# Moving three quarters of the second layer's routing beside the next block, with a ring of two weight strips in place of three

## The chip, the cores and the metric

The kernel runs on one core of one Trainium2 chip. The metric is device time in microseconds (us) of one execution; the median of three timed runs before the change is 1821.57 us (1821.03 to 1824.02).

## The reference

A two-layer decoder trunk on 256 tokens of width 1024, all in float32. Layer 0 mixes tokens with RWKV-7 and mLSTM heads; layer 1 with causal forgetting attention of 16 heads. Each layer is followed by PEER, an expert retrieval. For a block of 128 tokens it computes:

```
q  = (xb @ w_q)                      # 8 heads, two halves of 128
s1 = q half 1 . sub_k1 ; s2 = q half 2 . sub_k2    # 128 scores each
v1,i1 = top16(s1); v2,i2 = top16(s2)
sc,ci = top16(all 256 sums v1+v2)    # 16 experts a head, 128 a token
gate  = softmax(sc)
act   = gelu(xb . u_tab[expert])
out   = sum(gate * act * v_tab[expert])
```

The tables hold 16384 experts; a row of u and the same row of v stand side by side in memory, 2 x 1024 floats. Each of the 128 tokens of a block needs 128 such rows.

## The kernel before, in words

Five instruction streams run beside each other, ordered by semaphores, each written out in the order in which its engine works.

**Expert rows.** There are four expert passes, n = 0 to 3 (layer 0 blocks 0 and 1, layer 1 blocks 0 and 1), of 128 slots each. For each slot POOL issues one indirect DMA (L542) that brings one (u, v) row for each of the 128 tokens: 128 partitions x 8 KB, 1 MB, into a ring of 11 slots. DVE multiplies the u half with the tokens and sums (`Stream.dot`, L1700); ACT makes gelu, weight and a diagonal matrix of it (`Weights.pair`, L1201 to L1214); PE multiplies the diagonal matrix with the v half and adds into PSUM (`Experts.row`, L893), and by that frees the ring slot, for which POOL waits before it issues the row 11 further on. Each engine takes slots in pairs, by calls `ex.pairs(n)` that are strewn through the other work. PE runs one pair behind the count of ACT and DVE.

**Which pass runs beside what.** While layer 1's block b is mixed (`mixer1(b, ex)`, `mixer1_tail(b, ex)`), the pass n = 1 + b is streamed, that is the experts of the block before. The third, n = 3, runs alone at the end. In `mixer1` there is one pair for each of the 16 weight strips of q, k, v and the output gate, two pairs by the normalization of q and k ("rms"), and two for each of the eight attention steps. The tail has four pairs by the output projection, three at the layer norm, one at the first query strips, and three for each of four routing groups (`tail_pairs`); what is left of the 64 pairs goes in `finish()`.

**Routing.** `route(l, b, groups, between)` on DVE picks the experts. A group is two heads: top-16 of four score rows, 256 sums, top-16 again, indices by one-hot products, then `experts_chosen`, for which POOL's gather waits head by head. `between` is called at eight hooks of a group. ACT's counterpart is `gates` (an Exp for each group, after `gate_shifted`). Scores of all 16 half-heads of layer 1 go into `sc[:, 0]`, where they are read by `route`.

**Weights.** SP brings matrices as strips of 256 columns, 1 MB each, into the buffers of `wring`, WRING = 3 of them, used in turn. Strip i is loaded when the PSUM bank that was the last reader of strip i - WRING has been filled (L430). In layer 1 two strips fill one bank (`feature_strips`, `token_strips`): strip, pair, strip, bank filled, pair. So a bank's filling lets two loads go at once. In layer 0 most strips fill a bank of their own. `mixer0` begins the output projection with the mLSTM half of the rows of WRING strips before the RWKV half ("mixed") is ready; the transposes of the RWKV part stand before the last of them.

Of the kernel before, what the change touches and what calls it, by code (L numbers as in the profile page):

```python
# [58 lines left out]
PAIRS = tuple((2 * g, 2 * g + 2) for g in range(GROUPS))  # L59
FIRST_GROUPS = ((0, 1), (1, 2)) + PAIRS[1:]  # L60
# [17 lines left out]
def tail_pairs(g, hook):  # L78

    return int(hook in (0, 2, 5))  # L80
# [49 lines left out]
WRING = 3  # L130
# [68 lines left out]
def build(nc, T, out):  # L199
    ROWS, NROWS = parameter_rows()  # L200
    ctx = ExitStack()
    with ctx:
# [87 lines left out]
        ARENA = 36352  # L290
# [74 lines left out]
        keyT = cut(22528, 2048).rearrange("p (i n) -> p i n", i=16)  # L365
        qT = cut(24576, 4096).rearrange("p (i n) -> p i n", i=16)
        sc = cut(28672, 4096).rearrange("p (b i n) -> p b i n", b=NB, i=16)
        cand = cut(32768, 512).rearrange("p (h n) -> p h n", h=2)
        scr = cut(33280, 512)
        onehot = cut(33792, 512).rearrange("p (h k j) -> p h k j", h=2, k=TOPK)  # L370
        v16 = cut(34304, 64).rearrange("p (i k) -> p i k", i=4)
        i16f = cut(34368, 64).rearrange("p (h two k) -> p h two k", h=2, two=2)
        csc = cut(34432, 32).rearrange("p (h k) -> p h k", h=2)
        hilo = cut(34464, 64).rearrange("p (w h k) -> p w h k", w=2, h=2)
        e12 = cut(34528, 64).rearrange("p (w h k) -> p w h k", w=2, h=2)
        eidf = cut(34592, 32)
        gate = cut(34624, NB * SLOTS).rearrange("p (b s) -> p b s", b=NB)
        hid = cut(34880, NB * SLOTS).rearrange("p (b s) -> p b s", b=NB)
        ga = cut(35136, NB * SLOTS).rearrange("p (b s) -> p b s", b=NB)
        gsum = cut(35392, 2 * EH)  # L380
        uints = cut(35408, 416).bitcast(U32)
# [4 lines left out]
        diag = [cut(35840 + j * P, P) if j < 4 else early[:, (j - 4) * P:(j - 3) * P] for j in range(DIAGS)]  # L386
        qT1 = cut(24576, 2048).rearrange("p (i n) -> p i n", i=16)
# [3 lines left out]
        ogs = cut(24576, D)  # L391
        qc = cut(25600, 1024).rearrange("p (t n) -> p t n", t=8)
        kc = cut(26624, 2048).rearrange("p (t n) -> p t n", t=8)
        fv = cut(30720, 2048).rearrange("p (b n) -> p b n", b=NB)
        SQ = cut(28672, 2048).rearrange("p (t n) -> p t n", t=16)
        lg = cut(28672, 2 * 512).rearrange("p (j q n) -> p j q n", j=2, q=2)
        probT = cut(29696, 2 * 512).rearrange("p (j q s n) -> p j q s n", j=2, q=2, s=2)
        oT = cut(32768, D).rearrange("p (t n) -> p t n", t=KT)
# [153 lines left out]
        def _(pe):  # L552
# [25 lines left out]
            def mixer0():  # L578
# [192 lines left out]
                w = next_strip(pe)  # L771
                done(project_out(claim(pe, "mix_out", WRING), w, range(0, KT), True, True), "mix_out")
# [195 lines left out]
            def mixer1_tail(b, ex):  # L968
# [16 lines left out]
                for g in range(GROUPS + 1):  # L985

                    def between(j):
                        for i in (range(0, 2), range(2, 4))[j]:
                            ex.pairs(tail_pairs(g - 1, i) if g else QUERY_PAIRS * (i == 0))

                    if g < GROUPS:
                        k = EH + 1 + 4 * b + g
                        feature_strips("peer_q", k, b, between)
                        pe.wait_ge(S("peer_q_taken"), k + 1)
                        ps = claim(pe, "peer_s", k).rearrange("p (q n) -> p q n", q=4)
                        done(score_keys(ps, 0, range(4 * g, 4 * g + 4), lambda j: qT1[:, j, :]), "peer_s")
                        first_hook = 4
                    else:
                        first_hook = 0
                    if g:  # L1000
                        for i in range(first_hook, 8):
                            ex.pairs(tail_pairs(g - 1, i))
# [18 lines left out]
        def _(act):  # L1021
# [205 lines left out]
            def gates(n, groups, meanwhile):  # L1227

                for g, (h0, h1) in enumerate(groups):
                    for i in range(6):  # L1230
                        meanwhile(g, i)
                    gates_begun[0] += 1
                    act.wait_ge(S("gate_shifted"), gates_begun[0])
                    x = gate[:, n % NB, TOPK * h0:TOPK * h1]
                    af(x, x, ACT.Exp).then_inc(S("gate_exp"), 1)
                    for i in range(6, 8):
                        meanwhile(g, i)

            def mixer1(b, ex):
                tok = slice(b * P, (b + 1) * P)  # L1240
                wide = lambda ps: ps.rearrange("p (t n) -> p t n", n=P)
                take_x(4 + 4 * b, b)
                taken(af(fz, full(act, "fox_f", b)[:, 0:P], ACT.Identity, bias=small[:, 2:3], scale=1.0), "fox_f")
                ex.pairs(EARLY_PAIRS)
                for i in range(4):
                    ex.pairs(strip_pairs(2 * i))
# [9 lines left out]
                    ex.pairs(strip_pairs(2 * i + 1))  # L1256
                for i in range(2):
                    ex.pairs(strip_pairs(8 + 2 * i))
                    taken(copy(fv[:, b, i * 512:(i + 1) * 512], full(act, "fox_v", 2 * b + i)), "fox_v")
                    ex.pairs(strip_pairs(9 + 2 * i))  # L1260
                for i in range(12, 15):
                    ex.pairs(strip_pairs(i))
                for i in range(2):
                    taken(af(ogs[:, i * 512:(i + 1) * 512], full(act, "fox_og", 2 * b + i), ACT.Sigmoid), "fox_og")
                ex.pairs(strip_pairs(15))
# [25 lines left out]
            def mixer1_tail(b, ex):  # L1291
# [12 lines left out]
                def take_scores(g):  # L1304
                    ps = full(act, "peer_s", EH + 1 + 4 * b + g).rearrange("p (q n) -> p q n", q=4)
                    taken(copy(sc[:, 0, 4 * g:4 * g + 4, :], ps), "peer_s")

                def meanwhile(g, i):
                    ex.pairs(tail_pairs(g, i))
                    if g + 1 < GROUPS and i == 1:  # L1310
                        take_queries(g + 1)
                    if g + 1 < GROUPS and i == 3:
                        take_scores(g + 1)
# [4 lines left out]
                gates(2 + b, PAIRS, meanwhile)  # L1318
# [15 lines left out]
            ln_root(6)  # L1334
            ex.finish()
# [4 lines left out]
        def _(dve):  # L1340
# [277 lines left out]
            y_scratch = cut(25088, 1024)  # L1618
# [25 lines left out]
            def route(l, b, groups, between):  # L1644
# [10 lines left out]
                for g, (h0, h1) in enumerate(groups):  # L1655
# [6 lines left out]
                    top16(sc[:, 0 if l else b, js, :], scratch[:, 0:2 * nh, :], v16[:, 0:2 * nh, :], i16[:, 0:2 * nh, :], 2 * nh,  # L1662
# [83 lines left out]
            def mixer1(b, ex):  # L1746

                for i in range(2):
                    ex.pairs(strip_pairs(i))
                dve.wait_ge(S("fox_f_taken"), b + 1)  # L1750
                stt(fl, fz, -1.0, fz, ALU.mult, ALU.max).then_inc(S("f_abs"), 1)
                for i in range(2, 16):
                    ex.pairs(strip_pairs(i))
# [34 lines left out]
            def mixer1_tail(b, ex):  # L1788
# [10 lines left out]
                route(1, b, PAIRS, lambda g, i: ex.pairs(tail_pairs(g, i)))  # L1799
# [24 lines left out]
            layer_norm(6)  # L1824
            ex.finish()
# [50 lines left out]
```

## Time and profile before

| what | us |
|---|---|
| median of the timed runs | 1821.57 |
| the profiled execution | 1815.61 |
| its span, first to last instruction | 1813.6 |
| PE busy | 1551.5 |
| DVE busy | 1063.3 |
| ACT busy | 606.0 |
| POOL busy | 576.3 |

The page gives 40 slices of 45.3 us with the bytes moved in each. Expert rows are moved from about 325 us to about 1790 us. Layer 1's block 0 is mixed from about 680 us and its tail routes until about 1060 us; block 1 follows from about 1085 us to about 1465 us; the last pass takes the rest. SP's waits appear as SPq; a gather's issue has POOL's name.

### The profile page before, as it was taken

How to read it: one execution, taken by the hardware profiler on the slowest of the kernel's cores; microseconds unless marked ns; L12 is line 12 of the kernel's file. 1: busy time of each engine (PE TensorE's matmuls, PEld its weight loads, DVE VectorE, ACT ScalarE, POOL GpSimd, SP SyncE). 2: the span in 40 equal slices, each digit the busy share in tenths (PEclk: the TensorE clock that was granted, in tenths of full speed). 3: DMA queues.
4: the chain of work that ended last, by engine and by line, in shares of the span. 5: the costliest groups of instructions: out<-in, count | busy, mean ns of one | idle time of the engine just before them, and what ended most of it. 6: DMA issues, size and time to landing. Idle time of an engine off the chain costs nothing.

```text
span 1813.6 us, 18606 instructions
## 1 busy us (share of the span) xinstructions
PE 1551.5 (86%) x6020; PEld 927.1 (51%) x6020; DVE 1063.3 (59%) x2499; ACT 606.0 (33%) x1760; POOL 576.3 (32%) x561
## 2 busy tenths in 40 slices
PE   8999988998777778997899789998999787777775
PEld 7779877664222225753457436654557433222222
DVE  1683544577888865335557984325557985444444
ACT  1434311333333333236532332246632332222222
POOL 2000000344444442333332352234542354333330
PEclk9999859999999999999999999999999899999999
DMA  6222003999999999999999989999999899999996
GB/s 245 94 93 70 1 24 126 380 413 420 419 420 419 420 420 420 419 420 420 419 418 418 407 345 419 419 419 420 419 419 419 347 357 420 420 420 420 419 421 269
DMA packets 92063, 638.32 MB, mean 352 GB/s; under 512 B 11072, under 2 KB 13120, under 8 KB 15424
## 3 DMA queue, kind: packets, MB, share of 16 engines
q0 software_dynamic: 73728, 536.90, 71.9%
q1 hardware_dynamic: 18240, 100.24, 14.1%
q8 instruction: 49, 0.80, 0.2%
q14 instruction: 46, 0.38, 0.1%
HBM read 636.05 MB, written 1.05 MB: 351 GB/s over the span
## 4 chain that ended last, share of the span: by engine, by line
PE 45%; DMA 32%; DVE 15%; ACT 6%; issue 2%; POOL 0%; ACTq 0%; SPq 0%; DVEq 0%; POOLq 0%
DMA arena<-l_peer_uv,arena 31%; PE psum L893 19%; PE psum L575 12%; DVE arena L1700 6%; PE psum L874 4%; DMA wring<-l_w_in 2%; PE psum L752 1%; PE psum L797 1%; PE psum L668 1%; DVE arena L1639 1%; DVE arena L1630 1%; PE psum L658 1%; DVE arena L1631 1%; PE psum L667 1%; DVE arena L1635 1%
## 5 line engine op out<-in xcount | busy, mean ns | idle before, releaser
L542 POOL DMA_INDIRECT arena<-l_peer_uv,arena x512 | 563.1, 1100 | 1124.8 <-PE psum L893 870.2
L1700 DVE CUSTOM_DVE_ANT_0 arena<-arena,xres 128x1024 f32<-128x1024 f32 x512 | 617.8, 1222 | 454.8 <-DMA arena<-l_peer_uv,arena 452.3
L893 PE MATMUL psum<-arena,early 128*128 128x512 f32 x1024 | 487.9, 622 | 115.5 <-ACT early L1214 112.9
L893 PE MATMUL psum<-arena 128*128 128x512 f32 x1024 | 480.7, 615 | 100.5 <-ACT arena L1214 94.7
L893 PEld LDWEIGHTS psum<-arena,early 128*128 128x128 f32 x1024 | 193.6, 197 | 380.4 <-issue 205.4
L893 PEld LDWEIGHTS psum<-arena 128*128 128x128 f32 x1024 | 192.0, 195 | 360.0 <-issue 215.8
L575 PE MATMUL psum<-xT,wring 128*128 128x128 f32 (+2 forms) x1856 | 296.5, 320 | 13.8 <-DMA wring<-l_w_in 8.4
L575 PEld LDWEIGHTS psum<-xT,wring 128*128 128x128 f32 (+1 forms) x1856 | 269.2, 191 | 55.2 <-issue 23.2
L1201 ACT ACTIVATE arena<-arena 128x2 f32<-128x2 f32 x256 | 52.0, 203 | 646.7 <-DVE arena L1700 646.4
L1206 ACT ACTIVATE arena<-arena 128x1 f32<-128x1 f32 x512 | 123.2, 287 | 24.0 <-ACT arena L1201 0.4
L1029 ACT COPY arena<-psum 128x256 f32<-128x256 f32 (+2 forms) x138 | 62.5, 472 | 192.0 <-PE psum L575 85.9
L1214 ACT ACTIVATE arena<-ident,arena 128x128 f32<-128x128 f32 x256 | 86.9, 387 | 0.0
L1214 ACT ACTIVATE early<-ident,arena 128x128 f32<-128x128 f32 x256 | 86.9, 387 | 0.0
L874 PE MATMUL psum<-wring,xT 128*128 128x256 f32 x256 | 58.2, 380 | 0.3 <-DMA wring<-l_w_in 0.2
L874 PEld LDWEIGHTS psum<-wring,xT 128*128 128x128 f32 x256 | 48.4, 190 | 14.8 <-issue 6.2
L1201 ACT ACT_TABLE_LOAD x42 | 53.9, 1283 | 0.7
L1626 DVE MAX8 arena<-arena 128x8 f32<-128x128 f32 (+1 forms) x96 | 26.1, 326 | 38.3 <-ACT arena L1029 30.9
L1700 DVE DVE_READ_ACCUMULATOR2_ANT arena<- 128x1 f32 x512 | 42.1, 82 | 0.0
L1248 ACT ACTIVATE arena<-psum 128x512 f32<-128x512 f32 x8 | 4.8, 597 | 87.8 <-PE psum L575 87.8
L1782 DVE CUSTOM_DVE_ANT_0 arena<-psum,causal_ts 128x128 f32<-128x128 f32 (+1 forms) x32 | 10.2, 355 | 40.4 <-PE psum L943 40.4
L1630 DVE FIND_INDEX8 arena<-arena 128x8 uint32<-128x128 f32 (+1 forms) x96 | 31.5, 328 | 0.0
L752 PE MATMUL psum<-wring,arena 128*128 128x256 f32 x128 | 30.9, 404 | 0.7 <-DVEq L1602 0.7
(236 smaller groups left out, 1133.9 us busy)
## 6 DMA issues: line engine op xcount, KB each, us to landing
wring<-l_w_in SPq DMA_DIRECT2D x47, 1024.0 KB
wring<-l_peer_wq SPq DMA_DIRECT2D x24, 1024.0 KB
wring<-l_w_out SPq DMA_DIRECT2D x12, 1024.0 KB
arena<-l_peer_uv,arena POOLq DMA_INDIRECT x512
ln_par<-l_ln_g SPq DMA_DIRECT2D x6, 512.0 KB
ln_par<-l_ln_b SPq DMA_DIRECT2D x6, 512.0 KB
arena<-l_peer_keys SPq DMA_DIRECT2D x2, 1024.0 KB, 7.0
xT<-x_t SPq DMA_DIRECT2D x1, 1024.0 KB, 4.9
```

Source lines behind the costliest of these rows:

```text
L542: pool.indirect_dma_start(out=ring[:, g % RING, :], out_offset=None, in_=T[f"l{l}_peer_uv"], in_offset=bass.IndirectOffsetOnAxis(ap=eid[:, ...
L575: last = mm(ps, w[:, k, c0:c0 + cols], xT[:, k, tok], start=(k == 0), stop=(k == KT - 1))
L752: last = mm(ps[:, b * STRIP:(b + 1) * STRIP], yT[:, k, b * P:(b + 1) * P], w[:, k, :], start=first and (b, k) == (0, ks[0]), stop=end and ...
L874: last = mm(ps[:, i * STRIP:(i + 1) * STRIP], lhs(kt), w[:, kt, :], start=(kt == 0), stop=(kt == KT - 1))
L893: last = mm(self.ps[c], diag[k % DIAGS], ring[:, g % RING, D + c * 512:D + (c + 1) * 512], start=not self.begun, stop=True, skip_group_che ...
L1029: return nc.scalar.copy(out_, in_)
L1201: af(ga[:, self.b, 2 * p:2 * p + 2], hid[:, self.b, 2 * p:2 * p + 2], ACT.Gelu).then_inc(S("gelued"), 1)
L1206: af(w, w, ACT.Copy, scale=gate[:, self.b, s:s + 1]).then_inc(S("weights"), 1)
L1214: af(diag[k % DIAGS], ident[:], ACT.Copy, scale=ga[:, self.b, s:s + 1]).then_inc(S("diags_made"), 1)
L1626: st.then(v.max(vals[:, i, 0:8], src[:, i, :]))
L1630: st.then(v.max_index(idx[:, i, 0:8], vals[:, i, 0:8], src[:, i, :]))
L1700: v.tensor_tensor_reduce(out=u, in0=u, in1=xres[:, self.b, :], scale=1.0, scalar=0.0, op0=ALU.mult, op1=ALU.add, accum_out=hid[:, self.b, ...
```

## The change

- WRING goes from 3 to 2. The arena in SBUF grows by the 2048 columns of the freed buffer, and layer 1's scores get a place of their own, `sc1`. Everything behind the ring is laid out anew; the ring of rows keeps 11 slots.
- The tail of layer 1's block b routes only the first group of two heads (FIRST_PAIR). The six other heads (LATER, three groups) are routed in the next block's `mixer1`, in the place of the 16 plain pairs beside the weight strips (block 1), or beside pass n = 3 (after block 1), with one pair at each hook.
- In the tail six of the eight hooks have a pair (before three in each of four groups). PE's tail has one pair for each strip of the query projection but the second. ACT takes queries and scores of the later groups at these hooks.
- In `mixer1(1)` 16 of the 24 hooks have a pair; ACT's Exps of the three groups stand after 4, 10 and 15 of the pairs.
- `mixer0` begins two output strips instead of three before "mixed", and does two whole ones after.

```diff
+FIRST_PAIR, LATER = PAIRS[:1], PAIRS[1:]
-def tail_pairs(g, hook):
-    return int(hook in (0, 2, 5))
+def tail_pairs(hook):
+    return int(hook in (0, 1, 2, 4, 5, 6))
+def routed_pairs(g, hook):
+    return int((8 * g + hook) % 3 != 2)
+def pairs_before_exp(g):
+    return sum(routed_pairs(j, i) for j in range(g + 1) for i in range(8 if j < g else 6))
-WRING = 3
+WRING = 2
-        ARENA = 36352
+        ARENA = 38400
+        behind = lambda at, n: cut(RING * 2 * D + at, n)
+        sc1 = behind(0, 2048).rearrange("p (i n) -> p i n", i=16)
...
-            load_strips(16 + 3 - 3)
+            load_strips(16 + WRING - 3)
-            load_strips(3)
+            load_strips(6 - WRING)
...
# PE, mixer0
-                w = next_strip(pe)
-                done(project_out(claim(pe, "mix_out", WRING), w, range(0, KT), True, True), "mix_out")
+                for i in range(WRING, 4):
+                    w = next_strip(pe)
+                    done(project_out(claim(pe, "mix_out", i), w, range(0, KT), True, True), "mix_out")
# PE, mixer1_tail
-                for g in range(GROUPS + 1):
...
+                pumps = iter([QUERY_PAIRS, 0] + [1] * sum(tail_pairs(i) for i in range(8)))
+                for g in range(GROUPS):
+                    k = EH + 1 + 4 * b + g
+                    feature_strips("peer_q", k, b, lambda j: ex.pairs(next(pumps)))
...
# ACT
+                held = LATER if b else ()
+                def strip_step(i):
+                    ex.pairs(strip_pairs(i))
+                    for g, (h0, h1) in enumerate(held):
+                        if pairs_before_exp(g) == i + 1:
+                            gate_exp(2, h0, h1)
...
-                gates(2 + b, PAIRS, meanwhile)
+                gates(2 + b, FIRST_PAIR, meanwhile)
...
+            gates(3, LATER, lambda g, i: ex.pairs(1))
# DVE, mixer1
+                def meanwhile(g, i):
+                    ex.pairs(routed_pairs(g, i))
+                    if (g, i) == (0, 4):
+                        decay_sizes()
+                if b:
+                    route(1, 0, LATER, meanwhile)
+                else:
+                    for i in range(16):
+                        ex.pairs(strip_pairs(i))
...
# DVE, mixer1_tail and the end
-                route(1, b, PAIRS, lambda g, i: ex.pairs(tail_pairs(g, i)))
+                route(1, b, FIRST_PAIR, lambda g, i: ex.pairs(tail_pairs(i)))
...
+            route(1, 1, LATER, lambda g, i: ex.pairs(1))
```

## Rows read from the trace of the kernel before

**Rows 1.** The page, part 2: PE clock, DMA share and GB/s in 40 slices.
```profile
PEclk9999859999999999999999999999999899999999
DMA  6222003999999999999999989999999899999996
GB/s 245 94 93 70 1 24 126 380 413 420 419 420 419 420 420 420 419 420 420 419 418 418 407 345 419 419 419 420 419 419 419 347 357 420 420 420 420 419 421 269
```
**Rows 2.** The page, part 4: shares of the chain that ended last.
```profile
PE 45%; DMA 32%; DVE 15%; ACT 6%; issue 2%; POOL 0%; ACTq 0%; SPq 0%; DVEq 0%; POOLq 0%
```
**Rows 3.** Windows: stretch, length, PE, PEld, DVE, ACT, POOL busy, PEclk, DMA share, GB/s.
```profile
440.00:640.00 200.00, 148.61 (x312) 58.00 (x312) 166.49 (x478) 61.17 (x210) 86.52 (x79) 0.97 1.01 420
1000.00:1080.00 80.00, 62.00 (x177) 30.47 (x176) 72.50 (x218) 27.35 (x82) 30.80 (x27) 0.89 0.94 370
1400.00:1480.00 80.00, 63.66 (x194) 32.22 (x193) 75.47 (x233) 28.29 (x83) 32.03 (x25) 0.89 0.90 341
1500.00:1780.00 280.00, 209.41 (x453) 81.51 (x451) 138.10 (x224) 70.20 (x277) 109.68 (x113) 1.00 1.01 420
```
**Rows 4.** The chain of waits: one dot pair of each of three routing groups.
```profile
967.28 2.28 DVE arena L1700 x4
...
989.87 2.28 DVE arena L1700 x4
...
1012.51 2.28 DVE arena L1700 x4
```
**Rows 5.** The chain of waits beside weight strips: start us, us, what.
```profile
704.13 3.57 PE psum L575 x32
707.70 3.44 PE psum L893 x8
711.14 3.57 PE psum L575 x32
714.71 3.44 PE psum L893 x8
...
749.77 10.42 DMA wring<-l_w_in
```
**Rows 6.** Timeline, block 0's first query bank: start us, us, what, [idle before <-releaser].
```profile
963.95 14.41 SPq L430 DMA_DIRECT2D wring<-l_peer_wq  x4
...
973.03 3.84 PE L575 MATMUL psum<-xT,wring 128*128 128x128 f32 x32 [0.27 <-DMA wring<-l_peer_wq]
```
**Rows 7.** The page, part 6: the kernel's first transfer, KB, us to landing.
```profile
xT<-x_t SPq DMA_DIRECT2D x1, 1024.0 KB, 4.9
```
**Rows 8.** Windows of seven strip pairs in block 0 and in block 1.
```profile
707.70:805.70 98.00, 97.70 (x434) 66.91 (x433) 30.99 (x51) 25.27 (x88) 31.05 (x28) 1.00 1.01 419
...
1113.60:1211.20 97.60, 97.59 (x433) 66.89 (x433) 31.67 (x51) 25.06 (x88) 29.62 (x28) 1.00 1.01 419
```
**Rows 9.** Timeline of POOL: gathers issued after its longest waits for a slot.
```profile
824.61 1.21 POOL L542 DMA_INDIRECT arena<-l_peer_uv,arena  x1 [7.43 <-PE psum L893]
...
916.50 0.94 POOL L542 DMA_INDIRECT arena<-l_peer_uv,arena  x1 [9.06 <-PE psum L893]
...
971.32 0.94 POOL L542 DMA_INDIRECT arena<-l_peer_uv,arena  x1 [9.76 <-PE psum L893]
...
1323.32 0.94 POOL L542 DMA_INDIRECT arena<-l_peer_uv,arena  x1 [10.19 <-PE psum L893]
```
**Rows 10.** The chain of waits in block 1's attention: the same place of two steps.
```profile
1262.77 3.65 PE psum L893 x8
...
1273.06 3.65 PE psum L893 x8
```
**Rows 11.** Timeline of PE: layer 0's output projection, before and after "mixed".
```profile
264.38 9.72 PE L752 MATMUL psum<-wring,arena 128*128 128x256 f32 x32
...
279.10 17.53 PE L752 MATMUL psum<-wring,arena 128*128 128x256 f32 x80 [0.67 <-DVEq L1602]
```
**Rows 12.** Timeline of PE: an expert pair after an idle stretch.
```profile
820.55 6.36 PE L893 MATMUL psum<-arena 128*128 128x512 f32 x8 [4.58 <-ACT arena L1214]
```

More of the change, by code:

```diff
@@ L380, in build @@
-        gsum = cut(35392, 2 * EH)
-        uints = cut(35408, 416).bitcast(U32)
+        behind = lambda at, n: cut(RING * 2 * D + at, n)
+        sc1 = behind(0, 2048).rearrange("p (i n) -> p i n", i=16)
+        keyT = behind(2048, 2048).rearrange("p (i n) -> p i n", i=16)
+        qT = behind(4096, 4096).rearrange("p (i n) -> p i n", i=16)
+        sc = behind(8192, 4096).rearrange("p (b i n) -> p b i n", b=NB, i=16)
+        cand = behind(12288, 512).rearrange("p (h n) -> p h n", h=2)
+        scr = behind(12800, 512)
@@ new lines, in build @@
+        onehot = behind(13312, 512).rearrange("p (h k j) -> p h k j", h=2, k=TOPK)
+        v16 = behind(13824, 64).rearrange("p (i k) -> p i k", i=4)
+        i16f = behind(13888, 64).rearrange("p (h two k) -> p h two k", h=2, two=2)
+        csc = behind(13952, 32).rearrange("p (h k) -> p h k", h=2)
+        hilo = behind(13984, 64).rearrange("p (w h k) -> p w h k", w=2, h=2)
+        e12 = behind(14048, 64).rearrange("p (w h k) -> p w h k", w=2, h=2)
+        eidf = behind(14112, 32)
+        gate = behind(14144, NB * SLOTS).rearrange("p (b s) -> p b s", b=NB)
@@ L382, in build @@
+        hid = behind(14400, NB * SLOTS).rearrange("p (b s) -> p b s", b=NB)
+        ga = behind(14656, NB * SLOTS).rearrange("p (b s) -> p b s", b=NB)
+        gsum = behind(14912, 2 * EH)
+        uints = behind(14928, 416).bitcast(U32)
         i16 = uints[:, 0:64].rearrange("p (i k) -> p i k", k=TOPK)
@@ L385, in build @@
         eid = uints[:, 160:416].rearrange("p (b s) -> p b s", b=NB)
[L386 to L398, printed above, removed]
+        diag = [behind(15360 + j * P, P) if j < 4 else early[:, (j - 4) * P:(j - 3) * P] for j in range(DIAGS)]
+        qT1 = behind(4096, 2048).rearrange("p (i n) -> p i n", i=16)
+        ogs = behind(4096, D)
+        qc = behind(5120, 1024).rearrange("p (t n) -> p t n", t=8)
+        kc = behind(6144, 2048).rearrange("p (t n) -> p t n", t=8)
+        fv = behind(10240, 2048).rearrange("p (b n) -> p b n", b=NB)
+        SQ = behind(8192, 2048).rearrange("p (t n) -> p t n", t=16)
+        lg = behind(8192, 2 * 512).rearrange("p (j q n) -> p j q n", j=2, q=2)
+        probT = behind(9216, 2 * 512).rearrange("p (j q s n) -> p j q s n", j=2, q=2, s=2)
+        oT = behind(12288, D).rearrange("p (t n) -> p t n", t=KT)
         fz, fl, fc = mr[:, 0, 0:P], mr[:, 0, P:SEQ], mr[:, 1, :]
@@ L984, in mixer1_tail @@
                 pe.wait_ge(S("keys_loaded"), 32)
-                for g in range(GROUPS + 1):
[L987 to L1002, printed above, removed]
+                pumps = iter([QUERY_PAIRS, 0] + [1] * sum(tail_pairs(i) for i in range(8)))
+                for g in range(GROUPS):
+                    k = EH + 1 + 4 * b + g
+                    feature_strips("peer_q", k, b, lambda j: ex.pairs(next(pumps)))
+                    pe.wait_ge(S("peer_q_taken"), k + 1)
+                    ps = claim(pe, "peer_s", k).rearrange("p (q n) -> p q n", q=4)
+                    done(score_keys(ps, 0, range(4 * g, 4 * g + 4), lambda j: qT1[:, j, :]), "peer_s")
             mixer0()
@@ L1231, in gates, with gate_exp @@
                         meanwhile(g, i)
[L1232 to L1235, printed above, removed]
+                    gate_exp(n, h0, h1)
                     for i in range(6, 8):
                         meanwhile(g, i)
+            def gate_exp(n, h0, h1):
+                gates_begun[0] += 1
+                act.wait_ge(S("gate_shifted"), gates_begun[0])
+                x = gate[:, n % NB, TOPK * h0:TOPK * h1]
+                af(x, x, ACT.Exp).then_inc(S("gate_exp"), 1)
             def mixer1(b, ex):
@@ L1245, in mixer1 @@
                 for i in range(4):
-                    ex.pairs(strip_pairs(2 * i))
+                    strip_step(2 * i)
                     ps = wide(full(act, "fox_qk", 4 * b + i))
@@ L1255, in mixer1 @@
                         taken(last, "fox_qk")
[L1256 removed]
+                    strip_step(2 * i + 1)
                 for i in range(2):
[L1258 removed]
+                    strip_step(8 + 2 * i)
                     taken(copy(fv[:, b, i * 512:(i + 1) * 512], full(act, "fox_v", 2 * b + i)), "fox_v")
[L1260 removed]
+                    strip_step(9 + 2 * i)
                 for i in range(12, 15):
[L1262 removed]
+                    strip_step(i)
                 for i in range(2):
                     taken(af(ogs[:, i * 512:(i + 1) * 512], full(act, "fox_og", 2 * b + i), ACT.Sigmoid), "fox_og")
[L1265 removed]
+                strip_step(15)
                 act.wait_ge(S("f_abs"), b + 1)
@@ L1305, in take_scores @@
                     ps = full(act, "peer_s", EH + 1 + 4 * b + g).rearrange("p (q n) -> p q n", q=4)
-                    taken(copy(sc[:, 0, 4 * g:4 * g + 4, :], ps), "peer_s")
+                    taken(copy(sc1[:, 4 * g:4 * g + 4, :], ps), "peer_s")
+                taking = iter([(take_queries, 1), (take_scores, 1), (take_queries, 2), (take_scores, 2), (take_queries, 3),
+                               (take_scores, 3)])
                 def meanwhile(g, i):
[L1309 to L1313, printed above, removed]
+                    if tail_pairs(i):
+                        ex.pairs(1)
+                        take, g = next(taking)
+                        take(g)
                 ex.pairs(QUERY_PAIRS)
@@ L1661, in route @@
                     dve.wait_ge(S("peer_s_taken"), EH + 1 + GROUPS * b + h1 // 2 if l else 1 if (b, h1) == (0, 1) else h1 + 1)
-                    top16(sc[:, 0 if l else b, js, :], scratch[:, 0:2 * nh, :], v16[:, 0:2 * nh, :], i16[:, 0:2 * nh, :], 2 * nh,
+                    top16(sc1[:, js, :] if l else sc[:, b, js, :], scratch[:, 0:2 * nh, :], v16[:, 0:2 * nh, :], i16[:, 0:2 * nh, :], 2 * nh,
                           meanwhile)
@@ L1746, in mixer1, with decay_sizes @@
             def mixer1(b, ex):
[L1748 to L1753, printed above, removed]
+                def decay_sizes():
+                    dve.wait_ge(S("fox_f_taken"), b + 1)
+                    stt(fl, fz, -1.0, fz, ALU.mult, ALU.max).then_inc(S("f_abs"), 1)
+                def meanwhile(g, i):
[7 more added lines that the diff above has]
+                        ex.pairs(strip_pairs(i))
+                        if i == 2:
+                            decay_sizes()
                 ex.pairs(RMS_PAIRS)
```

17 lines of the change are left out of this document (1 added, 16 removed).

## The prediction

> **What bounds the kernel now.** I read the slices first. From slice 8 on the DMA engines are busy nearly without a break at 419 to 421 GB/s, save for two dips, slices 22 and 23 (407 and 345) and 31 and 32 (347 and 357) [rows 1]. So from 325 us to the end the kernel is bound by bytes: every microsecond in which the DMA engines move nothing is a microsecond of the end. The chain of waits gives PE 45% and DMA 32% [rows 2]; that PE leads must not mislead, since in these stretches PE and DMA run at nearly the same rate and the chain picks whichever came last. A row or a strip is 1,048,576 bytes, at 420 GB/s 2.50 us; this is my unit for what follows.
>
> Then I read windows. Two long ones hold 420 GB/s, 440 to 640 us, where DVE routes layer 0's second block with one pair at each hook, and 1500 to 1780 us, the last pass alone. The two that hold the tails' routing hold 370 and 341 [rows 3]. The dips are DVE's: 72.5 and 75.5 of 80 us busy. A routing group takes 22.6 us (989.87 - 967.28, and 1012.51 - 989.87) and has three pairs in it, of 2.28 us and a little each [rows 4]; so it frees 6 slots in 22.6 us, while the DMA engines could bring 9. As long as query strips are there to load, the engines have other bytes to move; when they run out, they starve.
>
> **The gain.** Idle in the dips is (420 - 370)/420 x 80 = 9.5 us and (420 - 341)/420 x 80 = 15.0 us, together 24.5 us [rows 3]. After the change a tail has one group. Its routing work is 22.6 - 3 x 2.37 = 15.5 us, with six pairs 15.5 + 14.2 = 29.7 us, 4.9 us a pair, as fast as the DMA engines bring two rows (5.0). The next pairs come free of routing. The three later groups of block 1 go beside the last pass, at one pair a hook, which is the pattern that holds 420 GB/s between 440 and 640 us: cost nothing. Those of block 0 go beside block 1's strips: 3 x 15.5 = 47 us more for a DVE that is busy 31.7 of 97.6 us there [rows 8]; cost nothing, since pairs wait for PE rather than for DVE. Were that cover gone, each group could hold PE for the longest stretch between two pairs, some 6 us. So the whole 24.5 us is to be had; bounds 18 and 24.5.
>
> **The strips of layer 1, what two buffers cost.** Before, PE works strip 3.57, pair 3.44, strip 3.57, pair 3.44, in all 14.0 us for two strips and four rows [rows 5], in which the DMA engines need 6 x 2.50 = 15.0 us. PE is busy 97.7 of 98.0 us [rows 8] and pulls the ring's queue deeper, by 7 x 1.0 = 7 us over the seven pairs of strips. This is possible because with three buffers the first strip after a filled bank is already there. With two it isn't: strips j and j+1 both wait for the bank that j-2 and j-1 fill together. PE does the one pair that stands there, 3.44 us, and then waits until strip j has landed. Let T be the time from filled bank to landed strip; then two strips take T + 3.57 + 3.44 + 3.57 = T + 10.6 us. Where does T lie? From below: a first transfer of 1 MB with nothing else under way took 4.9 us [rows 7]. From above: with the gathers' queue full, the first strip after the bank at 963.95 us was usable at 973.03, 9.1 us [rows 6], and a later one took 10.4 [rows 5]. With 9.1 PE would take 19.7 us for 15.0 us of transfers; the ring fills, the gathers' queue empties, and T falls. With 4.9 it is 15.5 and the DMA engines are still not full. So it settles between, near the lower end: when the ring is full, only the rows freed just before the bank are in the strip's way. I take T = 5.8, one such row's remainder on top of 4.9. That makes 16.4 us against 15.0, 1.4 us of idle for each filled bank. There are seven in a row in each block; one is paid by what the queue holds. 2 x 6 x 1.4 = 16.8 us; ends 2 x 6 x 0.5 = 6 and, at T = 7.5, 37. Beyond this the gap decides all the rest, because it takes away the queue's depth.
>
> A rule of the Trainium skill bears on T. The page DMA: Bandwidth & Descriptors, section Queues, rings and completion order, says that each DMA engine takes turns between the queues that have work, packet by packet. By it a strip against a full gather queue gets half the rate, which adds 2.5 us to the 4.9 alone and gives 7.4; the trace has 9.1, so the rule's direction agrees and its size is short. By 7.4 the strips' term would be 36 us instead of 16.8, if the gathers' queue stayed full.
>
> **Pauses that the depth covered.** Where PE frees no slot for long, POOL's waits show it: 7.43 us after block 0's strips (the normalization of q and k), 9.06 and 10.19 before the output projection, 9.76 at the first query bank [rows 9]. Before, the DMA engines were never idle in them, since they worked off the queue. Now they come to the first with an empty one. From the last bank of the strips they have one residue (3.2 us), two strips (5.0) and two rows (5.0) until about 13 us later, the next two rows only until 18, and the next slot is free at 18.9, its bytes 3.5 us behind: 4 us idle in each block, 8 in all (ends 0 and 14). In block 0's attention the DMA engines regain a queue; in block 1's they can't, because a step takes PE's chain 10.3 us [rows 10] for 10.0 us of rows: 0.3 x 8 = 2.4 us. At the output projection there are two strips ready instead of three, so the third makes PE wait too; with the pause ahead of it I count 4 us in block 0 and 7 in block 1. At the first query bank the third strip stood ready before; now PE waits T for it and the pause of 9.76 grows to some 16 us, with two strips and little else to move: 6 us, twice. Together 4 + 7 + 12 = 23 us (ends 6 and 35). The other two query gaps of each block cost as the strips' do, 2 x 2 x 1.4 = 5.6 us (ends 2 and 12).
>
> **Layer 0.** Its strips fill a bank each and take about 7 us, more than the 4.9 of a transfer: no cost. In the output projection the 80 matmuls after "mixed" take 17.53 us, 0.219 each [rows 11]. Now the transposes stand one half strip (16 matmuls of the 32 in 9.72 us) earlier, so "mixed" comes 3.4 us sooner, at 275.7. After it: 32 matmuls 7.0 us; the third strip, let go when the first of them fills its bank at 279.2, lands 4.9 to 5.1 later at 284.2, 1.6 us of wait; 64 matmuls 14.0. End 298.3 instead of 296.6: +1.7 us (ends 0 and 7, if the transposes weren't earlier). This shifts the first gather.
>
> **The sum.** 16.8 + 8 + 2.4 + 23 + 5.6 + 1.7 = 57.5 us lost, 24.5 won: +33.0. On the profiled execution, 1815.61 us (span 1813.6 and 2.0 around it), this is 1848.6; the median of the runs stands 5.96 above it, so 1854.6 us. All lower ends together, 6 + 0 + 0 + 6 + 2 + 0, less 24.5, are -10.5; all upper ones, 37 + 14 + 2.4 + 35 + 12 + 7, less 18, are +89.
>
> **The rivals.**
> *The gap is swallowed (faster).* If the gathers' queue is short whenever a bank fills, T is 4.9 and the pauses find strips and rows enough; what remains is the lower ends, some 6 to 8 us, against 24.5: 1821.6 - 24.5 + 7 = 1804. For it: the strips and rows hardly meet when the ring is full. Against: below T = 4.4 the loss would vanish, but even the lone transfer took 4.9 [rows 7], and PE was busy 97.7 of 98 us [rows 8], so nothing of the wait is hidden. Chance 0.15. Between this and my forecast the two may cancel, 1818 to 1825: 0.05.
> *PE's clock falls.* After 4.58 us of idle the expert pair at 820.55 took 6.36 us instead of 3.44 at a granted clock of half, the 1.2 GHz level [rows 12, 5]. With T = 5.8 PE idles 2.4 us at a gap, and beside such idle stretches the clock was 1.00 between 1500 and 1780 us [rows 3]; with T at 9 it idles 5.7. If it fell at each of some 20 gaps, 20 x 2.9 = 58 us of PE time, most of it on the path: 1821.6 + 33 + 45 = 1900. Chance 0.08. The Trainium skill, TensorE: Matmul & The Clock Gate, section HAM oscillation, describes just this, waits for a DMA between bursts that throttle the array again each time.
> *The routing beside the strips holds PE.* ACT stands in its order at an Exp until DVE has shifted the gates, and what it then is late with is PE's diagonals. 3 groups x 6 us: 1873. Against: DVE would be busy some 79 of at least 112 us, and ring rows are dotted several slots ahead of PE there. Chance 0.10.
> *My forecast*, slower by 10 to 58 us: 0.62.
>
> The likeliest is 1855; its own range is 1832 to 1880. The 8-in-10 range reaches to the cancelling case and into the swallowed one: 1815 to 1880. A difference under 0.2% (3.6 us) can't be told from none here. Slower: 0.62 + 0.08 + 0.10 = 0.80; within: 0.05; faster: 0.15.
>
> **What would show it.** In the profile after, PE must wait for a strip (DMA wring) after each filled bank of layer 1, some 2.4 us a time and some 20 times; the slices beside the strips must fall from 420 to about 385 GB/s; the two dips of the tails must be gone or shallow, and the last pass stay at 420 with DVE busier. The period of two strips must be 16 to 17 us. The prediction is wrong if those slices hold 420, or if the waits for strips are there and the DMA engines stay full all the same; if the dips stay, the move doesn't do what it says.

## The result, and the profile after

The changed kernel takes 1922.45 us, the median of four runs (1917.28 to 1925.92); the kernel before takes 1821.3 us beside it (1819.67 to 1824.02). The ratio is 1.0551, with a 95% interval of 1.0520 to 1.0583. The forecast was 1855, the range 1815 to 1880: the sign is right, and the loss is three times the one predicted. The profiled execution has a span of 1918.0 us, against 1813.6. One of experiment 9's ten executions, at 3151 us, is a disturbed one and is left out of its ratio; no other was.

The slices of the page after, the clock and GB/s, beside those of before [rows 1]:
```profile
PEclk9999769999999998989998998999998999999999
GB/s 212 108 88 45 1 47 164 420 413 420 420 419 420 419 420 336 308 348 387 419 384 284 399 419 402 301 325 366 416 325 349 329 401 420 420 420 420 420 420 277
```
A slice is now 47.95 us. Where layer 1's weight strips are (slices 15 to 17 and 25 to 27), the DMA engines bring 301 to 366 GB/s in place of 419, and at the output projections and query strips (20 and 21, 29 to 31) 284 to 384. Where there are no strips (7 to 14, and 33 to 38) they bring 413 to 420, as before. The windows show the same; the last of them shows that the later groups of routing cost nothing beside the last pass. Columns as in [rows 3]:
```profile
712.00:854.00 142.00, 112.51 (x433) 77.66 (x433) 37.98 (x63) 24.73 (x88) 31.84 (x28) 0.88 0.84 331
998.00:1072.00 74.00, 58.40 (x326) 46.25 (x327) 28.45 (x86) 10.92 (x37) 12.83 (x13) 0.88 0.81 323
1072.00:1144.00 72.00, 62.30 (x160) 27.67 (x159) 43.09 (x72) 25.55 (x84) 38.38 (x32) 0.98 1.02 415
1161.80:1304.70 142.90, 109.58 (x433) 75.86 (x432) 76.54 (x224) 32.01 (x96) 30.80 (x28) 0.90 0.87 338
1600.00:1890.00 290.00, 215.93 (x464) 84.33 (x464) 186.42 (x427) 82.83 (x303) 116.56 (x113) 0.99 1.01 420
```
The first and the fourth answer to [rows 8]. There PE was busy 97.70 of 98.00 us at full clock; here the same seven pairs of strips take 142 us, PE is idle for 29.5 of them, and the granted clock is 0.88. The third is block 0's tail, where the dip of 370 GB/s was: it is gone, 415.

What PE waited for, by line and releaser: us in total, times, longest. L588 and L888 are the two helpers' strip matmuls.
```profile
PE psum L588 <- DMA wring<-l_w_in: 38.3, 8, 8.4
PE psum L888 <- DMA wring<-l_w_in: 33.4, 8, 5.0
PE psum L588 <- DMA wring<-l_peer_wq: 29.0, 6, 7.5
PE psum L888 <- DMA wring<-l_w_out: 10.1, 2, 5.8
```
That is 110.8 us in 24 waits. Two of them, 8.4 and 0.5 us, are for layer 0's first strips; the other 22, 101.9 us, are layer 1's: seven and seven beside the strips, two at the output projections, six at the query strips. Now some of them from near, in the chain of waits (start us, us, what); it answers to [rows 5]:
```profile
734.61 7.79 DMA wring<-l_w_in
...
742.54 6.03 PE psum L588 x32
748.57 3.44 PE psum L907 x8
752.01 3.58 PE psum L588 x32
...
755.61 6.66 DMA wring<-l_w_in
...
762.40 3.81 PE psum L588 x32
766.21 3.44 PE psum L907 x8
769.65 3.58 PE psum L588 x32
...
773.25 7.46 DMA wring<-l_w_in
```
At 734.60 the bank is full and SP issues the next strip; it is usable 7.8 us later; in that time PE does the one pair that stands there and idles. Then the strip behind the gap takes 6.03 us instead of 3.57. The eight banks of block 0's strips fill at 712.0, 734.6, 755.6, 773.2, 793.1, 813.3, 833.5 and 854.0 us: a period of 20.3 us, against 14.0 before and 16.4 predicted. Over its seven gaps T, from filled bank to usable strip, is 7.5 us in the mean (6.7 to 8.9), and the strip behind the gap takes 5.7. T + 10.6 + (5.7 - 3.57) is 20.2, the period. In block 1 the means are 8.0 and 5.3 us, the period 20.4. Not every gap slows its strip: the one at 762.40 above takes 3.81 us after 3.4 us of idle, and two more of the 22 take 3.7 and 3.8.

One gap in the timeline (start us, us, engine and what, idle before it and its releaser):
```profile
788.21 0.94 POOL L555 DMA_INDIRECT arena<-l_peer_uv,arena  x1 [9.05 <-PE psum L907]
...
789.93 1.10 POOL L555 DMA_INDIRECT arena<-l_peer_uv,arena  x1 [0.78 <-PE psum L907]
...
793.14 0.80 SPq L443 DMA_DIRECT2D wring<-l_w_in  x2
...
795.10 0.94 POOL L555 DMA_INDIRECT arena<-l_peer_uv,arena  x1 [4.07 <-PE psum L907]
...
801.02 5.38 PE L888 MATMUL psum<-wring,xT 128*128 128x256 f32 x16 [4.48 <-DMA wring<-l_w_in]
...
808.39 1.41 POOL L555 DMA_INDIRECT arena<-l_peer_uv,arena  x1 [10.64 <-PE psum L907]
```
The row requests at 788.21 and 789.93 are on their way when the strips are issued at 793.14, and those at 795.10 and just after join them. POOL's 10.64 us without a free slot, up to 808.39, are the other half of the stall: PE frees no row while it waits for the strip.

The engines' idle time, length x (420 - GB/s) / 420, summed over windows from the first gather on, is 122 us after and 26 before. The front adds 6.1: the first gather is issued at 327.07 us, not 320.97. Together these are 102 of the 104 us between the spans.

### The profile page after: what moved, and what is told of

Same layout as the page of the kernel before. It is cut to its first block, busy times and chain, and to the rows that moved or that the text cites. A ratio compares the mean times of both kernels' runs of the same rounds, so it can differ in the third digit from the quotient of the medians.

```text
span 1918.0 us, 18617 instructions
## 1 busy us (share of the span) xinstructions
PE 1577.4 (82%) x6020; PEld 954.5 (50%) x6020; DVE 1059.1 (55%) x2499; ACT 604.9 (32%) x1759; POOL 591.8 (31%) x561
## 4 chain that ended last, share of the span: by engine, by line
PE 47%; DMA 38%; ACT 6%; DVE 6%; issue 2%; POOL 0%; ACTq 0%; SPq 0%; POOLq 0%; DVEq 0%
DMA arena<-l_peer_uv,arena 28%; PE psum L907 18%; PE psum L588 14%; DMA wring<-l_w_in 6%; PE psum L888 5%; DMA wring<-l_peer_wq 3%; DVE arena L1717 3%; PE psum L765 1%; DMA wring<-l_w_out 1%; ACT L1204 1%; PE psum L811 1%; PE psum L681 1%; PE psum L671 1%; PE psum L680 1%; ACT early L1217 1%
## 5 line engine op out<-in xcount | busy, mean ns | idle before, releaser
L555 POOL DMA_INDIRECT arena<-l_peer_uv,arena x512 | 578.6, 1130 | 1210.2 <-PE psum L907 952.1
L907 PE MATMUL psum<-arena 128*128 128x512 f32 x1024 | 475.9, 610 | 96.9 <-ACT arena L1217 96.9
L907 PE MATMUL psum<-arena,early 128*128 128x512 f32 x1024 | 471.8, 605 | 96.7 <-ACT early L1217 96.7
L588 PE MATMUL psum<-xT,wring 128*128 128x128 f32 (+2 forms) x1856 | 318.7, 336 | 71.2 <-DMA wring<-l_w_in 38.3
L907 PEld LDWEIGHTS psum<-arena,early 128*128 128x128 f32 x1024 | 187.7, 191 | 351.7 <-issue 192.0
L588 PEld LDWEIGHTS psum<-xT,wring 128*128 128x128 f32 (+1 forms) x1856 | 289.9, 207 | 112.6 <-issue 84.0
L888 PE MATMUL psum<-wring,xT 128*128 128x256 f32 x256 | 72.0, 444 | 33.4 <-DMA wring<-l_w_in 33.4
L888 PEld LDWEIGHTS psum<-wring,xT 128*128 128x128 f32 x256 | 57.6, 228 | 53.3 <-issue 43.6
L888 PE MATMUL psum<-wring,arena 128*128 128x256 f32 x128 | 33.1, 418 | 11.5 <-DMA wring<-l_w_out 10.1
```

The source lines that it names most:

```text
L555: pool.indirect_dma_start(out=ring[:, g % RING, :], out_offset=None, in_=T[f"l{l}_peer_uv"], in_offset=bass.IndirectOffsetOnAxis(ap=eid[:, ...
L588: last = mm(ps, w[:, k, c0:c0 + cols], xT[:, k, tok], start=(k == 0), stop=(k == KT - 1))
L888: last = mm(ps[:, i * STRIP:(i + 1) * STRIP], lhs(kt), w[:, kt, :], start=(kt == 0), stop=(kt == KT - 1))
L907: last = mm(self.ps[c], diag[k % DIAGS], ring[:, g % RING, D + c * 512:D + (c + 1) * 512], start=not self.begun, stop=True, skip_group_che ...
```

## The experiments

Each kernel was timed beside the kernel before on the same chip, and ratios are to that. A difference between two other kernels is of their medians where no ratio is named. "The release" below means that the first strip of a layer-1 pair gives its buffer free with its own last matmul.

**1. Three strips, ten rows, with the moved routing.**
```
-WRING = 2
-RING = 11
-ARENA = 38400
+WRING = 3
+RING = 10
+ARENA = 36352
```
(with layer 0's strip counts and one scratch tile set to match.)

> Theory (the gap): the loss of 101 us lies in the wait for a strip behind every filled bank, and it needs two strip buffers. With three strip buffers and ten ring rows the routing of block 1 still moves, but the next strip has a pair of experts and a strip's matmuls more to land: the waits for the strips of 33 + 38 + 29 + 10 us go, the period of a bank in the strips falls from 20.3 us to about 15, and what is won is the two dips of the kernel before, 24.5 us, less the price of one ring row, 0 to 15 us: 1797 to 1812 us. Rival (the moved routing itself costs: its VectorE and SyncE work lies in the way of the gathers): the time stays over 1850 us, with the rows dotted late in the strips of block 1.

1806.11 us (1801.62 to 1808.97), ratio 0.9923 [0.9899, 0.9946]: faster than before. PE's waits for layer-1 strips are 0.7 us in all. As expected.

**2. The kernel before with two strips.**
```
-WRING = 3
+WRING = 2
```
(with the preloads and layer 0's output loop set to that number.)

> The kernel before with two strip buffers in place of three and nothing else: the routing stays where it was, and the ring keeps its eleven rows. Theory (the gap): strips 58 us, query strips and attention as in the changed kernel where they don't lie beside the routing's own VectorE work, output projection 16, front 6: 1880 to 1925 us, with the same first strips of 5.4 to 6.5 us behind each gap. Rival (the loss is of the moved routing): within 20 us of 1821.

1923.65 us (1920.0 to 1924.29), ratio 1.0572 [1.0553, 1.0591], which overlaps the changed kernel's [1.0520, 1.0583]. The buffer alone makes the whole loss. Its GB/s and waits:
```profile
GB/s 213 106 88 45 1 49 173 420 414 419 420 420 420 419 420 329 287 342 391 419 386 330 414 368 394 311 323 359 415 326 348 399 329 414 420 420 420 420 420 277
```
```profile
PE psum L575 <- DMA wring<-l_w_in: 35.2, 8, 8.4
PE psum L875 <- DMA wring<-l_w_in: 33.3, 8, 5.0
PE psum L575 <- DMA wring<-l_peer_wq: 18.8, 6, 7.4
PE psum L875 <- DMA wring<-l_w_out: 9.6, 2, 5.9
```
Each row but one is within some 3 us of the changed kernel's. Only the query strips wait less, 18.8 us against 29.0. The two times agree within their intervals, so where the strips starve, the moved routing gains next to nothing. The smaller wait may come from the routing that stays in this kernel's tail, beside the query strips; that is a reading of the waits, not a test.

**3. The changed kernel with the release.** SP waits for a semaphore that the first strip's last matmul raises, instead of for the bank:
```
+                    else:
+                        last.then_inc(S("half_used"), 1)
...
-                        await_filled(sp, strips[i - WRING][2], strips[i - WRING][3])
+                        if strips[i - WRING][4]:
+                            sp.wait_ge(S("half_used"), strips[i - WRING][4])
+                        else:
+                            await_filled(sp, strips[i - WRING][2], strips[i - WRING][3])
```


> The changed kernel, still two strip buffers, but the first strip of each pair in layer 1 gives its buffer free with its own last matmul, one strip and two pairs of experts (about 10.4 us) before the next bank is claimed. Theory (the gap is only the landing behind the bank): a strip lands in 7 to 9 us under load, so it is there when the bank is; the gap of 4 to 5 us and with it the slow first strip go, the period falls from 20.3 us to about 15, and the time to 1800 to 1830 us. The second strip of a pair, still freed at the end, must land in T less the first strip's 3.6 us less nothing else: if its landing takes over 7 us behind the bank, a wait of some 3 us stays ahead of the second strip, and the time is 1840 to 1860. Rival (two buffers of any kind starve): no change from 1922.

1809.88 us (1808.95 to 1810.64), ratio 0.9950 [0.9934, 0.9967]. Two buffers, eleven rows, and 112 us less than the changed kernel. Its page:
```profile
PEclk9999859999999999998999999998999999999999
GB/s 222 113 63 83 1 13 128 324 417 415 420 420 420 421 419 420 419 419 420 419 420 419 414 420 419 419 419 400 414 382 419 413 420 420 420 420 419 420 420 245
```
The waits are gone, and so is the fallen clock beside them. The chain shows why: the strips are needed 7 us apart, and each now has one strip and two pairs, 10.4 us of PE's work, between the release of its buffer and its own turn.
```profile
751.39 3.57 PE psum L594 x32
754.97 3.44 PE psum L917 x8
758.40 3.45 PE psum L896 x16
761.86 3.43 PE psum L917 x8
...
765.31 3.72 PE psum L896 x16
```
The landing itself did not get shorter: the page's part 6 gives a median of 9.1 us from issue to landing for the `l_w_in` strips of both layers here, and 7.9 in the changed kernel. It only stopped being waited for. The wait that the expectation feared ahead of the second strip, for a landing of over 7 us, did not come: that strip too has 10.4 us, not 7.

**4. A busy gap.** Fourteen calls of `mm` on a constant (28 matmuls in the trace, 3.3 us), written to the claimed bank before its first strip:
```
+                for _ in range(14):
+                    mm(ps[:, 0:P], ident[:], ident[:], start=True, stop=True)
                 for i in range(2):
                     w = next_strip(pe)
```


> The changed kernel with 14 matmuls of 128 columns (about 3.1 us) on a constant ahead of the first strip of each layer-1 pair, written to the claimed bank, which the strip's own first matmul starts afresh; they lie in the wait for the strip and keep TensorE busy there. Theory (landing and clock both): the granted clock stays at the higher level, the strip behind the gap takes 3.6 us in place of 5.4 to 6.5, and some 22 gaps give back 2.2 us each: 1922 less 48, or 1874 us; the landing of about 7.5 us is unchanged. Rival (the clock only fills time that the transfers need anyway): the waits grow by what the strips give back, 1922. Rival (the extra matmuls come on top): over 1922.

1898.33 us (1893.23 to 1909.84), ratio 1.0458 [1.0415, 1.0502]: below the changed kernel by 24 us (17 by the ratios), at most half of the 48 expected. The chain and the clock:
```profile
732.57 7.47 DMA wring<-l_w_in
...
740.09 3.84 PE psum L588 x32
743.92 3.44 PE psum L911 x8
747.36 3.59 PE psum L588 x32
...
750.96 7.46 DMA wring<-l_w_in
```
```profile
PEclk9999769999999999999999999999999999999999
```
The granted clock stays up from slice 6 on, the strip behind the gap takes 3.84 us, and T stays at 7.5. The eight banks of block 0's strips fill between 712.6 and 840.5 us, a period of 18.3 instead of 20.3. So at a gap the clock was worth the 2 us expected.

Why is the whole less than half of that? From filled bank to filled bank the 22 gaps do return 44 us: 14 and 13 beside the strips, 5 and 5 at the query strips, 4 and 3 at the output projections. Their strips take 33 us less, and the rest is shorter landings (T in block 1 is 7.6, not 8.0). But the edit also puts its matmuls ahead of six banks whose first strip had already landed, three in each block: the first of the strips, of the output projection and of the query strips. There no wait hides them, and they stand in the chain:
```profile
936.43 3.39 PE psum L888 x28
...
985.03 3.39 PE psum L874 x28
988.42 3.58 PE psum L588 x32
```
The six gapless stretches in which they stand are 2.4 to 3.7 us longer than in the changed kernel, 19 us together. That is the rival "the extra matmuls come on top", true at these six places. A kernel with the matmuls in the 22 gaps alone was not run.

**5. Both pairs of experts behind the filled bank**, PE's order alone, two buffers:
```
                     if i:
                         done(last, name)
-                    between(i)
+                        between(0)
+                        between(1)
```


> The changed kernel with two strip buffers and its releases as they are, but in layer 1 both pairs of experts stand behind the filled bank and ahead of the next strips, so that TensorE has about 6.9 us of work in the wait for the strip. Theory (the gap's cost is the exposed landing, and its clock): the wait falls from 7.5 to 0 to 3 us, the clock stays high, the period falls from 20.3 us to 15 or 16: 1805 to 1840 us. Rival (rows of the second pair aren't there yet, so that the wait only changes its name to the rows): above 1860.

1825.58 us (1822.29 to 1833.11), ratio 1.0042 [1.0025, 1.0059]. PE has 6.87 us of work where it had 3.44, and most of the strip's landing hides behind it. The strips are issued in twos as before, but now nothing stands between the two on PE, so the second can end a wait of its own. Start us, us, what:
```profile
740.05 3.85 PE psum L588 x32
...
743.92 9.52 DMA wring<-l_w_in
...
753.57 9.01 PE psum L588 x64
762.58 6.87 PE psum L909 x16
```
PE's waits for layer 1's strips fall from 102 us to 38, and the granted clock stays up. Work behind the bank does as expected, but a buffer freed earlier does better (ratio 0.9950).

**6. Three strips, ten rows, moved routing, release** (experiments 1 and 3 together).

> Three strip buffers, ten ring rows, the moved routing (1806 us), and the release of each strip's buffer with its own last matmul as in the run of two buffers that took 1810 us. Theory (a strip needs only to be there when the bank is): with three buffers it already is, so nothing is left to win: 1800 to 1808 us. Rival (the landing still ends a wait here and there, as in the query strips): 1790 to 1800.

1807.08 us (1803.66 to 1810.79), ratio 0.9936 [0.9912, 0.9959]: level with experiment 1, as the theory had it. Nothing in layer 1 waits for strips any more.

**7. The kernel before with the release** (edit of experiment 3).

> The kernel before with its three strip buffers and eleven rows, and each strip's buffer freed with its own last matmul. It waits for no strip behind a bank in the trace of before, so the theory expects no change: 1815 to 1822 us, within the noise of 1818.7. Rival (earlier strips take engine time from the gathers or give it back): 10 us either way.

1819.31 us, ratio 1.0016 [0.9995, 1.0038]: no difference, as expected. The release is worth 112 us with two buffers and nothing with three.

**8. The kernel before with ten rows.**
```
-RING = 11
+RING = 10
```


> The kernel before with ten ring rows in place of eleven. It prices one row: theory, the ring covers the claims of the four rows of a bank in either case and the gathers are bound by the bytes, so 0 to 10 us more, 1819 to 1829. If it costs 15 or more, the gain of the moved routing in the run with ten rows (1806 us) is that much larger than the 12 us that show.

1823.16 us, ratio 1.0016 [0.9997, 1.0035]. A ring row is worth less than can be told here, at most some 6 us by the interval. Against it, experiment 1, also with ten rows and three strips, is 0.93% lower: the moved routing wins 17 us. The dips of its GB/s row, and that of experiment 1 below it:
```profile
GB/s 243 94 83 79 1 23 118 353 392 419 419 420 419 419 420 415 419 419 420 419 417 418 412 343 419 420 420 419 419 415 419 338 362 418 420 420 420 420 420 268
```
```profile
GB/s 246 94 73 92 1 2 121 338 413 419 419 419 419 420 420 399 420 419 420 419 399 419 414 420 419 419 420 419 419 397 420 407 420 420 420 420 420 419 420 252
```
Experiment 8's slices 23, 31 and 32 (343, 338, 362) are filled in experiment 1. Shallow ones come in their place, 399 at slices 15 and 20, 397 at 29 and 407 at 31: some 8 us of the 24.5.

**9. The kernel before with two strips and the release.** Beside experiment 3 only the routing's place differs.

> The kernel before with two strip buffers, eleven rows and the release of the first strip of each layer-1 pair with its own last matmul: beside the run of the changed kernel with the same release (1809.9 us), only the place of block 1's routing differs. Theory (the moved routing wins the two dips of the kernel before, which the ring-ten pair 1806.1 and 1823.2 put at 17 us): 1822 to 1832 us. Rival (the move wins nothing, and the release alone does all): 1810.

1823.39 us, ratio 1.0027 [1.0012, 1.0042]; experiment 3 has 0.9950, so the move wins 0.77%, or 14 us, at equal buffers. The rival, that the release alone does all, falls.

**10. The release for all strips but the queries'** (experiment 3's wait, with `and strips[i - WRING][2] != "peer_q"`).

> The changed kernel with two strip buffers, each first strip of a layer-1 pair freed with its own last matmul, but not those of the query strips, which are freed as in the changed kernel. Theory (the engines' idle time by stage in the trace after: strips 58, query strips 33, output projection 16, attention 9): the queries' 33 us stay, less some 5 us that the strips ahead of them no longer leave: 1838 to 1845 us. Rival (the query strips' idle time was inherited from the rows that came late through the earlier stages): 1810 to 1820.

1835.12 us (1832.65 to 1836.5), ratio 1.0081 [1.0054, 1.0108]: 1.3%, or 24 us, above experiment 3, 3 to 10 us less than expected. So of the 112 us the query strips are worth 24, and the other strips with what hangs on them 88.
```profile
GB/s 219 115 70 70 1 24 115 351 416 417 420 420 419 420 420 419 419 420 420 419 420 329 360 420 419 419 420 419 420 419 325 352 421 420 420 420 419 420 420 270
```
```profile
PE psum L594 <- DMA wring<-l_peer_wq: 27.7, 6, 7.5
```
Only the four slices of the query strips are low (329 and 360, 325 and 352), and 27.7 us of waiting, nearly the changed kernel's 29.0, cost 24.

## Why the prediction was wrong

Its mechanism was right: after each filled bank of a row of strips in layer 1 PE waits for the next strip, the two buffers are the cause (experiment 2 alone gives the loss; 1 and 3 take it away by two different edits), the dips go and the last pass stays at 420 GB/s with DVE busier, 186 of 290 us. Of its signs the period (20.3 us for 16 to 17) and the rate beside the strips (301 to 366 GB/s for 385) were off, both to the worse side. The failed step is the size of "T" in the strips' term, taken as 5.8 us where 7.5 and 8.0 were measured, and that the slower clock behind each gap, 2 us a bank, stood outside the sum.

- **T.** The prediction took 5.8 us, near the lower end of 4.9 and 9.1, because "when the ring is full, only the rows freed just before the bank are in the strip's way". The timeline has two rows requested in the 5 us before the bank and two just behind it, not one row's remainder. That it is these which make up the 7.5 is a reading of the timeline; no run tests it, and the cause of T's size stays open. At a period of T + 10.6 this alone makes 18.1 us, as experiment 4 shows (18.3), 3.1 us of idle a bank instead of 1.4. The middle of the two ends, 7.0, would have been nearer than the argument that chose the lower one. The 7.4 that the prediction set aside came nearer still, but it was for a full queue of gathers; where that queue is full, in experiment 3, the landing takes 9.1.
- **The clock.** It was a rival of 0.08, on the ground that PE would idle only 2.4 us at a gap. With T at 7.5 it idles 4, and a strip behind such a gap mostly runs at the lower level for some of its way: 5.7 us in the mean instead of 3.57. The row that showed it, 6.36 us for a pair after 4.58 idle [rows 12], was read and priced, and made dependent on the very T that was off. Experiment 4 shows the clock's share at the gaps, 33 us in 22 of them, or 44 with the landings that it shortened; as a whole it returned 17 to 24, since 19 went back where its matmuls came on top. The rival's price, 45 us, was about right; its chance and its place outside the sum were not. The Trainium skill, page TensorE: Matmul & The Clock Gate, section HAM oscillation, tells of waits for a DMA between bursts of matmuls, after each of which the array starts slow again. The trace agrees at 19 of the 22 gaps (5.1 to 6.6 us for the strip) and not at the other three (3.7 to 3.8).
- **The strips' term**, 16.8 us with an upper end of 37, measured 58 (idle time in the two windows of strips above). Period 20.3 less 15.0 is 5.3 a bank, 3.1 by T and 2.2 by the clock; seven of them are 37, and block 0's window has 30 of them as idle time, because the engines move 7 us more of transfers in it than six a bank. The prediction had this as one gap of seven paid by the queue. Its upper end, 37, held T alone.
- **The pauses.** The pause of the normalization was priced at 8 us and cost 1.7. Attention was priced at 2.4 and cost 8.7. The output projection cost 15.8 instead of 11. The query strips, priced at 17.6 (12 and 5.6), cost 33 as idle time, and 24 by experiment 10. The idle times are from the windows of the changed kernel's trace, and no run took the first three apart.
- **Layer 0**, +1.7. The output projection of the changed kernel, which answers to [rows 11]:
```profile
268.50 5.80 PE L765 MATMUL psum<-wring,arena 128*128 128x256 f32 x16
...
279.31 7.17 PE L765 MATMUL psum<-wring,arena 128*128 128x256 f32 x32 [0.68 <-DVEq L1619]
288.21 14.08 PE L765 MATMUL psum<-wring,arena 128*128 128x256 f32 x64 [1.73 <-DMA wring<-l_w_out]
```
It starts 4.1 us later and "mixed" comes 0.2 later, so 3.9 earlier beside it, where 3.4 was said; the third strip's wait is 1.73, where 1.6 was said. The term holds. The other 4.1 us of the front lie ahead of it and were in no term. They come without a missing strip buffer too: experiment 8, which differs from before in the ring's length alone, issues its first gather at 326.73, and experiment 7, with the ring as before, at 320.73. From 60 to 80 us the granted clock is 1.00 before, 0.83 after and 0.74 in experiment 8, and the DMA engines bring 104, 52 and 52 GB/s. Experiment 4, whose front is the changed kernel's, has 1.00 there and its first gather at 324.40. These are single profiles, so a difference between executions isn't told from one between kernels; what brings it about stays open.
- **The gain**, 24.5 us ("bounds 18 and 24.5"), is 17 us by experiments 1 and 8 and 14 by 3 and 9, on paths where strips don't starve; in the changed kernel the dips are gone or shallow (415 GB/s in block 0's tail and 400 in block 1's, where 370 and 341 were), and yet the whole is only 0.2% under experiment 2, within the noise.
- **The routing holds PE** (0.10): it doesn't. Experiment 3 has the same routing beside the strips and 419 GB/s there.

With 58, 1.7, 8.7, 15.8, 33 and the front's 6.1, the 57.5 us lost had to be 123; less a gain of some 20 this is the measured loss. That 1922 lies near the 1900 of the clock's rival is no merit of the forecast, which gave it 0.08. A version that beats both kernels came out of it: the moved routing with three strips and ten rows, 1806 us; two strips, eleven rows and the release are within 4 us of it, 1810.

## What to carry to other kernels

A buffer is priced by the latest moment at which its reload can start, against the first moment at which it is needed: two buffers freed together behind a common event cost 112 us more here than the same two freed one by one. Those came within some 5 us of three buffers (experiments 3 and 1, 9 and before), and with three the early release changed nothing. Where a landing time lies between two rows and the consumer stalls on it, carry it in the sum as the loaded one, and add the slower clock behind the stall in the same term instead of as a rival, since both come from one cause. Put matmuls that only keep the clock up where PE would wait, and nowhere else. And before giving up a buffer to pay for a move, price the thing that could be given up instead: one ring row of eleven cost too little to measure here.

## What the runs showed of the hardware

A strip took longer to land when the engines were full, 9.1 us (experiment 3), than when they starved, 7.9 (the changed kernel); the kernel with the longer landings is the one that is 112 us faster. In gaps of 4 us, 3.3 us of work on a constant kept the clock at its upper level (0.974 against 0.945 in the mean) and T at 7.5, and gave back 2 us a gap, 44 in 22 gaps; the whole gained 17 to 24. The granted clock in layer 0 differs between the profiles of kernels that differ only in the ring (1.00 and 0.74 from 60 to 80 us), into which no row is brought before 320 us, and the first gather lies anywhere from 320.7 to 328.7 us in the twelve profiles: some 0.4%, which has to be known before a change of that size is explained.
